# A two-layer diffusion backbone in fp32: the opening's scales and shifts summed together, its first up weights loaded in pairs

## The chip, the cores and the metric

The kernel runs on one core of one Trainium2 chip. The metric is the device time of one execution in microseconds; lower is better. All matrix products are done in fp32 precision, each by three products of rounded parts: a high part (fp32r, what the engine rounds to) and a low part, the difference.

## The reference, cut to what matters

```python
for l in range(DEPTH):                       # DEPTH = 2, D_MODEL = 1024, D_FF = 2816
    mod_x = adaln_params(c, w_mod[l], b_mod[l])          # silu(c) @ w_mod + b_mod, 9 sections of 1024
    mod_c = adaln_params(c_ctx[None], w_mod[l], b_mod[l])
    x   = ffn_sublayer(x,   mod_x, 0, norm_w[l, 0], ffn1_w_up[l], ffn1_w_down[l])   # 256 latent tokens
    ctx = ffn_sublayer(ctx, mod_c, 0, norm_w[l, 0], ffn1_w_up[l], ffn1_w_down[l])   # 256 context tokens
    ...                                                  # retention and convolution branches, second FFN
return rmsnorm(x, final_norm_w)

def modulated_norm(h, w, mod, i):
    return rmsnorm(h, w) * (1.0 + mod[:, :, 3 * i + 1]) + mod[:, :, 3 * i]

def ffn_sublayer(h, mod, i, norm_w, w_up, w_down):
    y = modulated_norm(h, norm_w, mod, i)
    a, b = jnp.split(y @ w_up, 2, axis=-1)
    return h + 0.5 * mod[:, :, 3 * i + 2] * ((jax.nn.silu(a) * b) @ w_down)
```

Only the opening matters here: the norm's scale (section 1) and shift (section 0) of layer 0, which two vector-by-matrix products give, then `y`, then the first columns of `y @ w_up`.

## The kernel before

The program is straight-line code for five queues. Activations lie transposed: `H`, `XN` and `Y` hold 8 blocks `k` of 128 channels, each 512 columns wide (256 latent tokens, then 256 context tokens). `Y[:, k, 0]` is the high part, `Y[:, k, 1]` the low one. A "unit" is a block of 1024 x 128 weights (512 KB); unit `cc` of the up stage is column block `cc // 2` of the first or the second half of `w_up`, and sums into PSUM bank `cc`. SyncE loads a unit into `RAW`, ScalarE copies its high part to `HI` (line 1095), VectorE subtracts and writes `LO` over `RAW` (line 1560), and TensorE runs 24 matmuls, three for each `k`: HI by Y high, HI by Y low, LO by Y high. There are six slots for units.

The stage "ada" is the opening. SyncE issues the inputs, then 16 pieces of `w_mod` (`load_mod(b)`, line 568, 512 KB each) and the first four up units, in one queue. Four groups `g` cover two blocks `k` each; the pieces of group `g` are `4g` and `4g + 1` (scale) and `4g + 2` and `4g + 3` (shift). TensorE's `modulation(b)` (line 844) multiplies a piece by `SCW`, the activated condition widened by zeros, so that 128 rows hold four partial sums for two conditions. ScalarE's `rows_out` (line 1236) copies the rows of one section out of bank 4 or 5, TensorE's `columns` (line 854) sums and turns them into columns, and VectorE's `mods0` (lines 1790 and 1796) adds the bias and forms the scale `AMUL`. Then `y0` on ScalarE (line 1244) writes the high part of `Y` for both conditions, `y0_full` and `y0_low` on VectorE (lines 1806, 1813) the low part. `xn` (line 1819) multiplies `H` by the inverse root. `h_copy` (1250 on ScalarE, 1827 on VectorE) copies the turned inputs out of the eight banks, block 7 out of bank 3. `keep_clock(n)` (line 811) runs `n` matmuls of ones whose result nobody reads.

The order of each queue is written out by hand. On TensorE `first_units(ks, units)` (lines 868 and 872) runs blocks `ks` of some of the four units among the modulation pieces. Units 2 and 3 run their blocks 6 and 7 last, after units 0 and 1 are complete. After the opening comes the stage "up" with units 4 to 43; there ScalarE applies Silu to unit 0 (line 1292) before it rounds unit 4, and a unit's load waits until the last user of its slot is complete. Everything downstream (down projection, retention, convolution, second layer) is not touched.

## Time and profile before

| | |
|---|---|
| median of 3 runs | 2137.32 us (2135.09 to 2137.92) |
| the profiled execution | 2135.14 us |
| its span | 2133.4 us |
| TensorE busy | 2121.3 us (99%) |
| VectorE busy | 1431.6 us (67%) |
| ScalarE busy | 804.5 us (38%) |
| mean transfer rate | 149 GB/s |
| first matmul of unit 4 | 56.88 us |

All times within the execution are microseconds from the start of the span. A timeline row gives the start, the duration, the engine (PE is TensorE, PEld its weight loads, DVE is VectorE, ACT is ScalarE), the line, the operation with its output and input, and in brackets the idle time before it with what ended it. A fp32 matmul shows as two passes (x2), and the shown end of a matmul reaches beyond the start of the next, so spacing between starts is what a matmul costs. What lies between the span and the time of the execution, 1.7 us, is start and end outside the queues.

### The profile page before, as it was taken

The numbers are of one execution on the slowest core, as the hardware profiler recorded it, in microseconds if no ns is written. First come the engines' busy times: TensorE is split into PE (matmuls) and PEld (weight loads), VectorE is DVE, ScalarE is ACT, GpSimd is POOL, SyncE is SP. The second block draws the span as 40 slices with busy tenths as digits, with TensorE's granted clock in tenths as the row PEclk, the third lists the DMA queues.
The fourth block names the chain that finished last, engine by engine and source line by source line (L and its number), as shares of the span: only waits on it lengthen the run. The fifth ranks groups of instructions, "written<-read, shape, count | busy, mean of one in ns | idle before, by whom it ended". The sixth has DMA issues, their size and how long they took to land.

```text
span 2133.4 us, 26488 instructions
## 1 busy us (share of the span) xinstructions
PE 2121.3 (99%) x10747; PEld 1803.4 (85%) x10747; DVE 1431.6 (67%) x1965; ACT 804.5 (38%) x1194; POOL 0.2 (0%) x4
## 2 busy tenths in 40 slices
PE   9999999999999999999999999999999999999998
PEld 7888888988888888888888888888889888888887
DVE  5677777659588773477777767733335688777765
ACT  4322222455322322342222233222223665556654
POOL 0000000000000000000000000000000000000000
PEclk9999999999999999999999999999999999999999
DMA  8655555431555543355555544433333447775664
GB/s 262 197 170 175 160 166 161 126 99 41 157 158 158 172 154 99 89 149 163 172 168 161 169 135 144 133 98 99 92 99 107 133 116 199 206 212 144 188 190 146
DMA packets 454398, 318.17 MB, mean 149 GB/s; under 512 B 10478, under 2 KB 429702, under 8 KB 453894
## 3 DMA queue, kind: packets, MB, share of 16 engines
q1 hardware_dynamic: 432476, 243.43, 39.3%
q10 hardware_dynamic: 21800, 73.03, 10.0%
q8 instruction: 86, 1.41, 0.3%
q14 instruction: 36, 0.29, 0.0%
HBM read 312.23 MB, written 1.05 MB: 147 GB/s over the span
## 4 chain that ended last, share of the span: by engine, by line
PE 97%; SPq 1%; DVE 1%; DMA 0%; ACT 0%; issue 0%; DVEq 0%
PE bank L645 23%; PE bank L647 23%; PE bank L646 23%; PE bank L656 9%; PE bank L659 5%; PE bank L963 4%; PE bank L691 2%; PE bank L727 1%; PE bank L725 1%; PE bank L726 1%; PE bank L695 1%; SPq L568 1%; PE bank L868 1%; PE bank L801 0%; DMA RAW<-in_ffn_w_up_dram 0%; PE bank L1007 0%
## 5 line engine op out<-in xcount | busy, mean ns | idle before, releaser
L1560 DVE TENSOR_TENSOR LO<-RAW,HI 128x1024 fp32r<-128x1024 f32 (+1 forms) x435 | 523.1, 1207 | 341.0 <-ACT HI L1095 340.9
L645 PE MATMUL bank<-Y,HI 128*128 128x512 f32 (+1 forms) x1440 | 555.7, 386 | 0.0
L647 PE MATMUL bank<-Y,LO 128*128 128x512 f32 (+1 forms) x1440 | 553.6, 384 | 0.0
L646 PE MATMUL bank<-Y,HI 128*128 128x512 f32 (+1 forms) x1440 | 553.5, 384 | 0.0
L1095 ACT ACTIVATE HI<-RAW 128x1024 fp32r<-128x1024 f32 (+1 forms) x435 | 441.5, 1039 | 141.5 <-DMA RAW<-in_w_in_dram 52.2
L645 PEld LDWEIGHTS bank<-Y,HI 128*128 128x128 f32 x1440 | 270.6, 188 | 54.2 <-issue 1.3
L647 PEld LDWEIGHTS bank<-Y,LO 128*128 128x128 f32 x1440 | 270.5, 188 | 53.9
L646 PEld LDWEIGHTS bank<-Y,HI 128*128 128x128 f32 x1440 | 270.6, 188 | 53.6 <-issue 0.5
L1571 DVE SCALAR_TENSOR_TENSOR MODACC<-MODRAW,SC,MODACC 128x1024 f32<-128x1024 f32 x224 | 277.2, 1279 | 2.4 <-DMA MODRAW<-in_w_mod_dram 2.0
L645 PE MATMUL bank<-Z,HI 128*128 128x512 f32 (+1 forms) x594 | 218.0, 367 | 0.0
L647 PE MATMUL bank<-Z,LO 128*128 128x512 f32 (+1 forms) x594 | 217.1, 366 | 0.0
L646 PE MATMUL bank<-Z,HI 128*128 128x512 f32 (+1 forms) x594 | 217.1, 365 | 0.0
L1292 ACT ACTIVATE TMP<-bank 128x512 f32<-128x512 f32 x66 | 39.5, 598 | 457.0 <-PE bank L647 373.5
L656 PE MATMUL bank<-Y,HI 128*128 128x512 f32 x720 | 181.0, 393 | 0.0
L656 PEld LDWEIGHTS bank<-Y,HI 128*128 128x128 f32 x720 | 129.6, 189 | 23.3
L645 PEld LDWEIGHTS bank<-Z,HI 128*128 128x128 f32 x594 | 112.0, 189 | 18.2
L646 PEld LDWEIGHTS bank<-Z,HI 128*128 128x128 f32 x594 | 112.0, 189 | 18.1
L647 PEld LDWEIGHTS bank<-Z,LO 128*128 128x128 f32 x594 | 112.0, 189 | 17.9
L1680 DVE SCALAR_TENSOR_TENSOR H<-bank,GATE,H 128x256 f32<-128x256 f32 x64 | 28.3, 479 | 121.7 <-PE bank L647 121.7
L659 PEld LDWEIGHTS bank<-Y,LO 128*128 128x128 f32 x720 | 98.2, 190 | 7.0
L659 PE MATMUL bank<-Y,LO 128*128 128x256 f32 x720 | 100.4, 282 | 0.0
L1889 DVE TENSOR_TENSOR TMP<-bank,TMP 128x512 f32<-128x512 f32 x66 | 45.5, 690 | 75.7 <-PE bank L647 75.7
(290 smaller groups left out, 2468.2 us busy)
## 6 DMA issues: line engine op xcount, KB each, us to landing
RAW<-in_ffn_w_up_dram SPq DMA_DIRECT2D x174, 512.0 KB, 3.8
MODRAW<-in_w_mod_dram ACTq DMA_DIRECT2D x128, 512.0 KB, 4.4
RAW<-in_w_in_dram SPq DMA_DIRECT2D x128, 512.0 KB, 4.0
RAW<-in_ffn_w_down_dram SPq DMA_DIRECT2D x66, 512.0 KB, 3.9
RAW<-in_ffn_w_down_dram SPq DMA_DIRECT2D x24, 384.0 KB, 3.4
WM<-in_w_mod_dram SPq DMA_DIRECT2D x16, 512.0 KB, 8.3
RAW<-in_w_ret_out_dram SPq DMA_DIRECT2D x16, 512.0 KB, 4.1
RAW<-in_w_conv_out_dram SPq DMA_DIRECT2D x16, 512.0 KB, 4.0
```

Of the source, the lines that this page charges most:

```text
L645: mm(bank, hi, X[:, k, 0, cols], start=first, stop=False)
L646: mm(bank, hi, X[:, k, 1, cols], start=False, stop=False)
L647: return mm(bank, lo, X[:, k, 0, cols], start=False, stop=end)
L656: mm(halves2(bank[:]), wblock(u, 0, k), X[:, k, :, cols], start=(k == 0), stop=False)
L659: ins = mm(bank[:, 0:HALF], wblock(u, 1, k), X[:, k, 0, cols], start=False, stop=(k == KT - 1))
L691: mm(B[cc][:, cols], wblock(s.u + cc, part, k), Y[:, k, 0, cols], start=(k == 0 and part == 0), stop=False)
L963: ins = mm(B[s.acc[4 * half + tt].bank][:], Y[:, k, a, tt * P:(tt + 1) * P], weights(u, w)[:, kk * 512:(kk + 1) * 512], start=(k == 0 and ...
L1095: A(weights(v, 0), raw_weights(v), ACT.Copy).then_inc(hi_done, 1)
L1292: A(TMP[:, o % 2, cols], B[s.acc[cc].bank][:, cols], ACT.Silu).then_inc(drained[s.acc[cc].bank], 1)
L1560: V_.tensor_tensor(weights(v, 1), raw_weights(v), weights(v, 0).bitcast(F32), ALU.subtract).then_inc(lo_done, 1)
L1571: V_.scalar_tensor_tensor(acc, MODRAW[i % 2][:], a, acc, ALU.mult, ALU.add).then_inc(mod_step, 1)
L1889: V_.tensor_tensor(TMP[:, 2 + o % 2, cols], B[s.acc[cc].bank][:, cols], TMP[:, o % 2, cols], ALU.mult).then_inc(drained[s.acc[cc].bank], 1)
```

## The change

Six things change, all in the opening.

- Scale and shift of a group are summed in the same rows: `SCW` has a copy of the condition for each section, two columns apart, and all four pieces of a group accumulate in one bank (4 or 5 by turns). One `rows_out`, one `columns` (which yields four columns for each block) and one `mods0` serve a group.
- The first four up units are loaded as two pairs of 1 MB, (0, 2) and (1, 3). A pair holds two neighbouring column blocks of one half of `w_up`, 1 KB a row. The first pair is issued behind pieces 0 to 3, the second behind pieces 4 to 7. Low parts are written over the pair, with a stride.
- TensorE sweeps unit by unit: unit 0 and unit 2 on blocks 0 and 1, then pieces 4 to 7, then units 0, 2, 1 and 3 as listed; in `one_unit` all products with the high weights come first, then those with the low weights. Blocks 4 to 7 run over all four units together (`all_units`).
- In ScalarE's queue a unit's rounding stands between blocks of `y0`.
- In VectorE's queue the copies of blocks 5 and 7 and the second block's scaling stand behind the low part of block 0.
- The dummies: 3, 2, 2 and 8 in place of 3, 5, 3, 2 and 5. The wait for bank 3 stands before the last ones in both.

```diff
@@ plan
-            s.rows = [[p.acc(4), p.acc(5)] for g in range(4)]
-            s.cols_acc = [[p.acc(6), p.acc(7)] for g in range(4)]
+            s.rows = [p.acc(4 + g % 2) for g in range(4)]
+            s.cols_acc = [p.acc(7 - g % 2) for g in range(4)]
...
+    for i, pair in enumerate(PAIRS):                  # PAIRS = ((0, 2), (1, 3))
+        for e, u in enumerate(pair):
+            p.slot[u], p.prior[u], p.landed[u], p.pair[u] = u, None, 16, (i, e)
+        user[2 * i] = user[2 * i + 1] = pair[1]
@@ SyncE
-                    load_mod(0)
-                    load_mod(1)
-                    load_up(0)
...
-                    load_up(3)
+                    def load_pair(i):
+                        sp.dma_start(RAWP[i][:], wu.rearrange("(k p) n -> p k n", p=P)[:, :, i * FF:i * FF + 2 * P]
+                                     ).then_inc(raw_landed[2 * i], 16)
+                    for b in range(4):
+                        load_mod(b)
+                    load_pair(0)
+                    for b in range(4, 8):
+                        load_mod(b)
+                    load_pair(1)
                     for b in range(8, 16):
                         load_mod(b)
@@ TensorE
+                    def one_unit(cc, ks):
+
+                        n = [u for pair in PAIRS for u in pair].index(cc)
+                        if 0 in ks:
+                            bank_wait(pe, up_s.acc[cc])
+                            pe.wait_ge(hi_done, n + 1)
                         for k in ks:
                             pe.wait_ge(y0_hi, 2 * k + 2)
...
+                            mm(B[cc][:], wblock(cc, 0, k), Y[:, k, 0, :], start=(k == 0), stop=False)
                             pe.wait_ge(y0_lo, k + 1)
...
+                            mm(B[cc][:], wblock(cc, 0, k), Y[:, k, 1, :], start=False, stop=False)
+                        if 0 in ks:
+                            pe.wait_ge(lo_done, n + 1)
+                        for k in ks:
+                            ins = mm(B[cc][:], wblock(cc, 1, k), Y[:, k, 0, :], start=False, stop=(k == KT - 1))
...
                     modulation(0)
                     drain_wait(pe, s.turn[0])
                     keep_clock(3, s.turn[0].bank)
...
-                    columns(0, 1)
                     drain_wait(pe, s.turn[6])
-                    keep_clock(5, s.turn[6].bank)
                     modulation(2)
-                    keep_clock(3, s.turn[6].bank)
+                    keep_clock(2, s.turn[6].bank)
                     modulation(3)
                     keep_clock(2, s.turn[6].bank)
-                    columns(0, 0)
+                    columns(0)
                     drain_wait(pe, s.turn[7])
-                    keep_clock(5, s.turn[7].bank)
-                    first_units((0, 1), (0,))
...
-                    first_units((6, 7), (3,))
+                    keep_clock(8, s.turn[7].bank)
+                    one_unit(0, (0, 1))
+                    one_unit(2, (0, 1))
+                    for b in range(4, 8):
+                        modulation(b)
+                    columns(1)
+                    one_unit(0, (2, 3))
+                    one_unit(2, (2, 3))
+                    one_unit(1, (0, 1, 2, 3))
+                    one_unit(3, (0, 1))
                     for b in range(8, 12):
                         modulation(b)
...
+                    one_unit(3, (2,))
+                    columns(2)
+                    one_unit(3, (3,))
+                    all_units(4, range(4))
                     for b in range(12, 16):
                         modulation(b)
...
+                    all_units(5, (0, 1))
+                    columns(3)
+                    all_units(5, (2, 3))
+                    all_units(6, range(4))
+                    all_units(7, range(4))
@@ ScalarE
-                    h_copy(0, 1, 3)
...
-                    y0(5, 6, 7)
+                    h_copy(0, 1, 3, 6)
+                    rows_out(0)
+                    y0(0)
+                    pair_hi(0)
+                    y0(1)
+                    pair_hi(2)
+                    rows_out(1)
                     y0(2, 3)
...
+                    pair_hi(1)
+                    pair_hi(3)
+                    split_at[0] = 4
+                    rows_out(2)
+                    y0(4, 5)
+                    rows_out(3)
+                    y0(6, 7)
@@ VectorE
-                    xn(0, 1)
-                    mods0(0, 1)
-                    h_copy(5, 7)
-                    split_upto(0)
-                    mods0(0, 0)
+                    xn(0)
+                    mods0(0)
                     y0_full(0)
                     y0_low(0)
+                    xn(1)
+                    h_copy(5, 7)
+                    pair_lo(0)
                     y0_full(1)
                     y0_low(1)
-                    split_upto(2)
...
+                    pair_lo(2)
+                    xn(2, 3, 4, 5)
+                    mods0(1)
...
```

## Rows read from the trace of the kernel before

**Rows 1.** The page, part 1: busy time and share by engine.

```profile
PE 2121.3 (99%) x10747; PEld 1803.4 (85%) x10747; DVE 1431.6 (67%) x1965; ACT 804.5 (38%) x1194; POOL 0.2 (0%) x4
```

**Rows 2.** Busy by engine (instructions), clock, transfer share, GB/s, by stretch.

```profile
20.00:25.00 5.00, 4.25 (x24) 2.95 (x24) 4.30 (x9) 3.37 (x6) 0.00 (x0) 1.00 1.13 327
35.00:40.00 5.00, 5.00 (x45) 3.58 (x47) 3.58 (x7) 0.35 (x2) 0.00 (x0) 1.00 1.10 350
50.00:55.00 5.00, 5.00 (x24) 4.12 (x23) 1.65 (x3) 3.57 (x6) 0.00 (x0) 1.00 0.00 1
60.00:65.00 5.00, 5.00 (x24) 4.14 (x23) 3.00 (x5) 2.92 (x4) 0.00 (x0) 1.00 1.11 346
60.00:500.00 440.00, 439.97 (x2154) 373.37 (x2153) 317.91 (x411) 149.39 (x208) 0.00 (x0) 1.00 0.49 151
```

**Rows 3.** Chain of waits, opening: start, duration, what.

```profile
22.45 8.06 DMA RAW<-in_ffn_w_up_dram
...
30.54 1.06 ACT HI L1095
...
32.02 0.58 PE bank L854 x4
```

**Rows 4.** Timeline of TensorE, 19 to 57 us.

```profile
19.25 0.64 PE L844 MATMUL bank<-WM,SCW 128*32 128x256 f32 x8
...
20.49 0.58 PE L854 MATMUL bank<-CK,ADAROWS 128*128 128x2 f32 x4
20.93 1.36 PE L811 MATMUL bank<-ONES 128*128 128x128 f32 x10
22.59 0.47 PE L868 MATMUL bank<-Y,HI 128*128 128x512 f32 x1 [0.30 <-ACT Y L1244]
...
42.84 1.93 PE L844 MATMUL bank<-WM,SCW 128*32 128x256 f32 x32
44.71 0.50 PE L868 MATMUL bank<-Y,HI 128*128 128x512 f32 x1
...
53.50 0.62 PE L872 MATMUL bank<-Y,HI 128*128 128x512 f32 x2
...
56.44 0.39 PE L872 MATMUL bank<-Y,HI 128*128 128x512 f32 x1
56.88 0.47 PE L645 MATMUL bank<-Y,HI 128*128 128x512 f32 x1
```

**Rows 5.** Issues from 3.0 to 3.2 us in flight, median to landing.

```profile
WM<-in_w_mod_dram SPq DMA_DIRECT2D x2, 512.0 KB, 10.9
```

**Rows 6.** Timeline of VectorE, 10 to 22 us.

```profile
10.00 1.23 DVE L1821 SCALAR_TENSOR_TENSOR TMP<-XROWS 128x1024 f32<-128x1024 f32 x1 [2.63 <-DMA XROWS<-in_ctx_dram]
...
18.57 1.28 DVE L1827 COPY H<-bank 128x512 f32<-128x512 f32 x2
19.77 1.22 DVE L1560 TENSOR_TENSOR LO<-RAW,HI 128x1024 fp32r<-128x1024 f32 x1
21.10 0.16 DVE L1790 TENSOR_TENSOR MODS<-bank,VT 128x4 f32<-128x4 f32 x1
```

**Rows 7.** Timeline of ScalarE, 12 to 22 us.

```profile
12.03 1.55 ACT L1250 ACTIVATE H<-bank 128x512 f32<-128x512 f32 x3
...
21.35 2.08 ACT L1244 ACTIVATE Y<-XN,MODS,AMUL 128x256 fp32r<-128x256 f32 x4 [1.01 <-DVE MODS L1790]
```

**Rows 8.** Up loads issued from 50 to 70 us: issue to landing.

```profile
DMA to landing us min/median/max: 3.9/5.2/6.5
```

**Rows 9.** Columns as in the second group, the program's end.

```profile
2127.00:2128.00 1.00, 0.43 (x4) 0.23 (x2) 0.88 (x3) 0.51 (x2) 0.00 (x0) 1.00 0.00 0
...
2131.00:2132.00 1.00, 0.00 (x0) 0.00 (x0) 0.00 (x0) 0.00 (x0) 0.00 (x0) 0.77 1.02 381
```

**Rows 10.** Dummies' weight loads from 0.9 to 3.9 and 5 to 8 us.

```profile
L811 PEld LDWEIGHTS bank<-ONES x14: 288/333/333, 1.0 to 3.8; 128*128 128x128 f32 x14
...
L811 PEld LDWEIGHTS bank<-ONES x25: 186/192/290, 4.8 to 8.0; 128*128 128x128 f32 x25
```

More of the change, by code:

```diff
@@ L48, in constants @@
     keep[:, CK_QS:CK_QS + P] = (p[:, None] % 32 == p[None, :] % 32)
-    keep[p % 32 == 0, CK_COMB] = 1.0
-    keep[p % 32 == 1, CK_COMB + 1] = 1.0
+    for row in range(4):
+        keep[p % 32 == row, CK_COMB + row] = 1.0
     mix = np.zeros((P, CM_W), np.float32)
@@ L75 @@
 V_SPARE = (2, 4)
+PAIRS = ((0, 2), (1, 3))
 class Acc:
@@ L105, in __init__ @@
         self.total_acc = {}
-        self.slot, self.prior, self.landed = {}, {}, {}
+        self.slot, self.prior, self.landed, self.pair = {}, {}, {}, {}
     def acc(self, bank):
@@ L298, in plan @@
             u = s.u + c
+            if u in p.pair:
+                continue
             slot = (u + (rows and s.kind in ("up", "down"))) % SLOTS
@@ L361, in build @@
     CROWS = place("CROWS", [2 * KT, P], F32, zone + 82944)
[L362 to L363 removed]
+    ADAROWS = place("ADAROWS", [P, 2, GROUP], F32, zone + 83968)
+    SCW = place("SCW", [P, KT, 2, 32], F32, zone + 88064)
     DIAG = place("DIAG", [P, 512], F32, zone + 94208)
@@ L369, in build @@
     RAW = [place(f"RAW{s}", [P, UW], F32, cursor[0] + 4 * UW * s) for s in range(SLOTS)]
+    RAWP, LOP = [[place(f"{n}{i}", [P, KT, 2 * P], dt, cursor[0] + 8 * UW * i) for i in range(2)]
+                 for n, dt in (("RAWP", F32), ("LOP", F32R))]
     LO = [place(f"LO{s}", [P, UW], F32R) for s in range(SLOTS)]
@@ L460, in weights @@
             slot = pl.slot[u]
+            if u in pl.pair:
+                i, e = pl.pair[u]
+                return (HI[slot][:].rearrange("p (k n) -> p k n", k=KT), LOP[i][:, :, e * P:(e + 1) * P])[part]
             if slot < SLOTS:
@@ L468, in wblock @@
             slot = pl.slot[u]
+            if u in pl.pair and part:
+                i, e = pl.pair[u]
+                return LOP[i][:, kk, e * P:(e + 1) * P]
             if slot < SLOTS:
@@ L480, in raw_weights @@
             slot = pl.slot[u]
+            if u in pl.pair:
+                i, e = pl.pair[u]
+                return RAWP[i][:, :, e * P:(e + 1) * P]
             if slot < SLOTS:
@@ new lines, in one_unit, with all_units @@
+                        if 0 in ks:
+                            pe.wait_ge(lo_done, n + 1)
+                        for k in ks:
+                            ins = mm(B[cc][:], wblock(cc, 1, k), Y[:, k, 0, :], start=False, stop=(k == KT - 1))
+                        if KT - 1 in ks:
+                            ins.then_inc(unit_done, 1)
+                    def all_units(k, units):
+                        pe.wait_ge(y0_hi, 2 * k + 2)
+                        for cc in units:
+                            for part in range(2):
+                                mm(B[cc][:], wblock(cc, part, k), Y[:, k, 0, :], start=False, stop=False)
+                        pe.wait_ge(y0_lo, k + 1)
+                        for cc in units:
+                            ins = mm(B[cc][:], wblock(cc, 0, k), Y[:, k, 1, :], start=False, stop=(k == KT - 1))
+                            if k == KT - 1:
+                                ins.then_inc(unit_done, 1)
@@ L1776, in _ @@
             dve.wait_ge(small_set, 4)
-            V_.tensor_copy(SCW[:, :, 0:2], SC[:].rearrange("p c k -> p k c")).then_inc(sc_wide, 1)
+            for sec in range(2):
+                V_.tensor_copy(SCW[:, :, sec, 2 * sec:2 * sec + 2], SC[:].rearrange("p c k -> p k c")).then_inc(sc_wide, 1)
             for s in stages:
@@ L1800, in y0_full, with pair_lo @@
+                    def pair_lo(cc):
+                        dve.wait_ge(hi_done, [u for pair in PAIRS for u in pair].index(cc) + 1)
+                        V_.tensor_tensor(weights(cc, 1), raw_weights(cc), weights(cc, 0).bitcast(F32), ALU.subtract
+                                         ).then_inc(lo_done, 1)
                     def y0_full(*ks):
                         for k in ks:
-                            drain_wait(dve, s.cols_acc[k // 2][0])
+                            dve.wait_ge(mods0_done, k // 2 + 1)
+                            dve.wait_ge(xn_done, k + 1)
```

152 lines of the change are left out of this document (48 added, 104 removed).

## The prediction, written before the change was run

> **What bounds the kernel now.** I read the busy shares first, then TensorE's clock and the transfers in five-microsecond stretches, then the chain of waits through the opening, and last the timelines of the three engines, one against another. TensorE is busy 99% of the span [rows 1], so nearly nothing is to be won outside the first 57 us, and whatever TensorE loses or gains there is passed on to the end at its full size: from 60 to 500 us it is idle for 0.03 us [rows 2]. In the opening the transfers run at 327 to 350 GB/s and are idle from 50 to 55 us, while TensorE works without a gap [rows 2]. So the opening is bound by transfers only in its first half. The chain says where it changes hands: the fourth up block lands at 30.5 us, is rounded and subtracted, and lets the second group's sums go on at 32.0 us [rows 3]. From 35 us on TensorE has no gap [rows 2] until 0.2 us before unit 4 begins at 56.88 us [rows 4]. The reader should see that the last transfers of the modulation weights are not what is waited for: TensorE comes to them at 42.84 us from other work, not from a wait.
>
> From 22.59 to 56.67 us TensorE spends 34.1 us. Of this, 96 matmuls of the first four units cost 96 x 0.227 = 21.8 us (thirteen steps from 53.50 to 56.44 are 0.226 each [rows 4], with the first of a group a little longer); twelve modulation pieces cost 12 x 0.465 = 5.6 (four take 1.87, from 42.84 to 44.71 [rows 4]); six turnings cost 6 x 0.44 = 2.6. The rest, about 4.1 us, is waiting. A change that removed all waiting and two turnings' worth could not bring much over 4 us; that is the whole prize.
>
> **The change, part by part.** I follow the new order with the old durations.
>
> Small edits first. SCW has twice the columns: one memset 0.27 us longer and one more copy of 0.18 on VectorE, which then idles 2.63 us for the context rows [rows 6]; nothing, and 0.45 us if that cover were gone. The number of weight transfers is the same; four blocks of 512 KB become two of 1 MB whose rows are twice as long. ScalarE writes out four sums in place of eight (0.38 us each), TensorE turns four times, which saves 4 x 0.44 = 1.8 us, 1.3 of it after the first unit begins. VectorE's small sums stay twelve.
>
> *Transfers.* All issues sit in SyncE's queue; no waiting instruction lies among them. Piece 3 now lands ahead of any up block, the first pair follows, pieces 4 to 7 come before the second pair. The mixed stretches run at 327 GB/s, the one with modulation weights alone at 350 [rows 2]; with a third of the bytes in up blocks that is 289 GB/s for an up block, 1.8 us against 1.5. But 60 to 65 us carries up blocks mainly and runs at 346. So a block in a pair costs between 1.5 and 1.8 us. The Trainium skill, "DMA: Bandwidth & Descriptors", Specifications, gives full rate from runs of 512 B upward; by it the pairs would win nothing, and the first mixed stretches here do not bear that out. Either way the first pair lands at 20.3 to 20.9 us: the first two pieces take 10.9 us from issue in the median [rows 5], so the second, issued at 3.1, is in at about 14.2, and two pieces of 1.5 and the pair follow. ScalarE asks for it only at 21.2: no effect on the sum.
>
> *The opening to the first scale.* The first piece now goes to bank 4, which ScalarE frees with its third copy at 13.58 [rows 7] rather than with its second, so it starts 0.5 us later, at 13.7. Then: 0.57 for the piece, 0.87 for three dummies, 0.57, then 0.96 for the broadcast of the inverse roots: piece 2 begins at 16.65 and piece 3 at 17.8, instead of 19.25, since five dummies and one turning are gone and it has landed (17.3). From piece 3's start to the first small sum took 1.85 us (19.25 to 21.10 [rows 4, 6]): 19.65. The three small sums end at 20.1. ScalarE writes the first Y at 20.2 (now 21.35 [rows 7]): 1.1 us gained.
>
> *The gap that this opens.* TensorE ends its only turning at 19.6. Its next instruction waits for bank 3, which VectorE frees with the copy of block 7. Today that copy is done at 19.8 [rows 6]. In the new order it stands behind the full and the low part of block 0 and the scaling of block 1. The low part waits for ScalarE's two halves, half of 2.08 us [rows 7], until 21.3. A pass of VectorE over 512 columns takes 0.6 to 0.7 us (two copies 1.28 [rows 6]). Low part, scaling and two copies, 2.5 us: bank 3 is free at 23.8. TensorE is idle from 19.6 to 23.9, 4.3 us. Then eight dummies, 16 passes of 0.136 us (ten take 1.36 [rows 4]), 2.2 us: the first unit begins at 26.1, not at 22.6. VectorE meanwhile goes on to unit 0's low weights (23.75, 1.14), block 1 full and low (0.66, 0.69): 26.2, unit 2's low weights to 27.4. So without the dummies unit 0 would still end only 0.4 us earlier; the order on VectorE holds it too. High parts first hides only the low weights, not block 1. Cost: 3.5 us in the start. Strided reads of a pair have no row; the engines take 1.06 and 1.22 us for 1024 elements in a row [rows 3, 6], and I take these; between 0 and +0.5 us.
>
> *The middle.* Units 0 and 2 on two blocks: 12 x 0.227, to 28.8. Pieces 4 to 7 (landed by 27): to 30.7. Sum out, turned, small sums: 30.7 + 0.1 + 0.38 + 0.1 + 0.6 + 0.5 = 32.4, then 1.0 on ScalarE for block 2, and TensorE has its block at 33.4. Idle 2.3 us, with no unit queued behind it. Unit 0 on blocks 2 and 3 waits for each part in turn, 1.4 us more. At 36.2 everything is there; unit 2 (1.4), unit 1 (2.7), unit 3 (1.4), pieces 8 to 11 (1.9): 43.5. Three matmuls, the turning at 44.2, three matmuls, 45.3. Block 4 is ready 2.2 us after its turning starts (0.6 to the first small sum as from 20.49 to 21.10, 0.5 for the three, 1.1 for ScalarE's two halves [rows 4, 6, 7]); today four pieces cover that. It waits to 46.4: 1.1 us. Twelve matmuls, pieces, half of block 5 and the last turning: 52.8. Half of block 5 covers 1.4 of the 1.8 us after it; 0.4 us idle. Blocks 6 and 7: the last matmul ends its turn at 60.1. Check as a sum: 26.1 + 21.8 + 5.6 + 1.3 + (2.3 + 1.4 + 1.1 + 0.4) = 60.0. Now it is 56.67: +3.4 us. Bounds of the four waits together: 1.2 us less (small handovers cost 0.1 rather than 0.4), 1 us more.
>
> *The end of the opening.* ScalarE rounds unit 4's weights only behind the Silu of unit 0, and VectorE subtracts behind that. From the start of unit 0's last matmul (53.50) to unit 4's first (56.88) is 3.4 us [rows 4]. Now twelve matmuls of units 2 and 3 lie in between and the gap is 0.2. In the new order all four units end together, three matmuls after unit 0: 0.9 us of cover from that start. TensorE is idle 2.5 us: +2.3 (1.9 to 2.7). The transfers of units 6 to 9 now wait for units 2 and 3, that is for 59.9 us; they take 3.9 to 6.5 us to land [rows 8], ScalarE and VectorE 2.3 more, and unit 6 is due 10.9 us after unit 4's start, at 73.5. Cover about 5 us; no cost, and 1 us of waiting for each us by which it is exceeded. The earlier table load on ScalarE (1.28) ends well before.
>
> Sum: +3.4 + 2.3 = +5.7 us. The profiled execution took 2135.14 us around its span of 2133.4; it would become 2140.8. The median of the three runs is 2137.32, 2.2 higher, so the forecast is **2143.0 us**, its own range +4.4 to +6.9 and 1 us of spread on both sides.
>
> **Rivals.** *The clock falls in the gap.* At the end of the program TensorE stops at 2127.4, and the granted clock over 2131 to 2132 is 0.77, so that it fell to 1.2 GHz about the middle of it, some 4.1 us after the last matmul [rows 9]. My gap is 4.3 us, good to some 0.3, hardly longer than that one, and matmuls that begin in time would keep the clock: a third of the cases in which the gap is there. At the program's start weight loads of dummies take 333 ns up to 3.8 us and 192 from 4.8 on [rows 10], the low level and 2.4 GHz, and 13 of them start between 1.0 and 3.8, 0.215 each. Sixteen dummy passes then cost 16 x 0.215 in place of 16 x 0.136, +1.3, and one unit matmul doubles: +1.5, in all +7.2, 2144.5. The Trainium skill, "TensorE: Matmul & The Clock Gate", Part 1, calls the half rate the state after idling; the end of the trace agrees.
>
> *Transfers set the opening after all.* If the last piece, not TensorE, holds the end of the opening, the end moves with its landing, 1.2 us earlier, and only the tail is paid: +1.1, 2138.4. A mixture (half of the gaps covered) gives +3. Against it: no TensorE gap after 35 us now.
>
> *Faster.* If bank 3 is free early and VectorE is not what holds block 1, the first unit starts with the first Y, at 21.4: 21.4 + 28.7 + 1.5 of waits = 51.6, plus 2.5 of tail = 54.1 against 56.88: -2.8, 2134.5. With no waits at all it is -4.3. It decides from where VectorE's copy of block 7 is done before 20 us; the diff puts it behind block 0. *The change doesn't do what it says*: the up blocks are needed so late that their order is without effect; it gives the transfers' case.
>
> **How the numbers follow.** A measurement can tell about 0.2%, 4.3 us. Forecast 0.43, clock 0.2, transfers or mixture 0.27, faster 0.10. Slower by over 0.2%: most of the first (0.39) and all of the second, 0.59. Within: 0.04 of the first, the third, and 0.05 of the faster case, 0.36. Faster: the other 0.05. The range goes from the transfers' case less 1 us of spread, 2137.3, to the clock case with its waits at their upper bound, 2146.5.
>
> **What would show it.** In the new profile: TensorE idle some 4 us before the eight dummies, released by VectorE's copy of H; first unit matmul near 26; gaps of about 2, 1 and 0.5 us before blocks 2, 4 and 6; unit 4 about 3.4 us after unit 0's last matmul starts, at 62.6; dummies of 16 passes in 2.2 us (3.4 if the clock fell). The forecast is wrong if bank 3 is free before 20 us, or if unit 4 begins before 60 us.

## The result, and the profile after

The changed kernel takes 2147.35 us in the median (2145.71 to 2148.07, six runs); the kernel before, on the same chip, 2135.72 (2135.09 to 2137.92). The ratio is 1.005, with a 95% interval of 1.004 to 1.006: slower by 11.6 us. The forecast was slower by 5.7 us, 2143.0; the sign and the places are right, the size is half of the measured one, and the measured median lies 0.85 us above the stated range. The forecast stood on a median of 2137.32 us for the kernel before; counted from there the range reached to +9.2 us, so in differences the measured 11.6 lies 2.4 us beyond it.

The profiled execution took 2145.71 us, its span 2143.9, 10.5 more than before. All of that is there when unit 4 begins: 67.41 us against 56.88 [rows 4], also 10.5. What follows lasts 2076.49 us, before 2076.52. TensorE's timeline of the opening (columns as ahead, L860 is the modulation, L870 the turning, L827 the dummies, L882 to L900 the first four units, L661 unit 4):

```profile
13.39 0.64 PE L860 MATMUL bank<-WM,SCW 128*32 128x256 f32 x8 [1.33 <-ACT H L1274]
...
17.66 0.64 PE L860 MATMUL bank<-WM,SCW 128*32 128x256 f32 x8
...
18.89 0.58 PE L870 MATMUL bank<-CK,ADAROWS 128*128 128x4 f32 x4
23.71 3.78 PE L827 MATMUL bank<-ONES 128*128 128x128 f32 x16 [4.24 <-DVE H L1857]
27.15 0.77 PE L882 MATMUL bank<-Y,HI 128*128 128x512 f32 x1
...
30.60 1.93 PE L860 MATMUL bank<-WM,SCW 128*32 128x256 f32 x32
33.12 0.58 PE L870 MATMUL bank<-CK,ADAROWS 128*128 128x4 f32 x4 [0.59 <-ACT ADAROWS L1257]
35.42 0.80 PE L882 MATMUL bank<-Y,HI 128*128 128x512 f32 x1 [1.72 <-ACT Y L1268]
...
39.04 0.63 PE L882 MATMUL bank<-Y,HI 128*128 128x512 f32 x1
...
41.60 0.52 PE L882 MATMUL bank<-Y,HI 128*128 128x512 f32 x1
...
45.95 1.93 PE L860 MATMUL bank<-WM,SCW 128*32 128x256 f32 x32
...
50.84 0.50 PE L897 MATMUL bank<-Y,HI 128*128 128x512 f32 x1 [0.90 <-ACT Y L1268]
...
59.37 0.50 PE L897 MATMUL bank<-Y,HI 128*128 128x512 f32 x1 [0.21 <-ACT Y L1268]
...
64.04 1.07 PE L900 MATMUL bank<-Y,HI 128*128 128x512 f32 x4
67.41 0.47 PE L661 MATMUL bank<-Y,HI 128*128 128x512 f32 x1 [2.31 <-DVE LO L1582]
```

The gap is where it was forecast: the turning stands at 18.89 [rows 4: 20.49], then TensorE idles 4.24 us, released by VectorE's copy of `H`. Three more gaps follow, before block 2 (1.72 us), block 4 (0.90) and block 6 (0.21), and one of 2.31 us before unit 4, released by `LO`. Two things are not in the forecast's main case. The dummies take 3.44 us to the next start where 16 x 0.136 = 2.2 were reckoned, and the six matmuls from 39.04 to 41.60 start 0.43 us apart where 0.227 was reckoned [rows 4].

The order on VectorE that holds bank 3 (L1857 copies blocks 5 and 7):

```profile
21.16 0.69 DVE L1843 TENSOR_TENSOR Y<-TMP,Y 128x512 fp32r<-128x512 f32 x1 [0.39 <-ACT Y L1268]
21.77 0.68 DVE L1849 TENSOR_TENSOR XN<-H,RB 128x512 f32<-128x512 f32 x1
22.38 1.28 DVE L1857 COPY H<-bank 128x512 f32<-128x512 f32 x2
23.57 1.22 DVE L1826 TENSOR_TENSOR LOP<-RAWP,HI 128x1024 fp32r<-128x1024 f32 x1
24.71 0.73 DVE L1836 TENSOR_SCALAR TMP<-XN,AMUL,MODS 128x256 f32<-128x256 f32 x2
25.54 0.69 DVE L1843 TENSOR_TENSOR Y<-TMP,Y 128x512 fp32r<-128x512 f32 x1
```

The copies end at 23.66, today's at 19.85 [rows 6]. The low part of block 1, on which unit 0's second block waits, ends at 26.2.

TensorE's clock, by stretch (columns as in [rows 2]; the clock is the number behind the POOL column):

```profile
20.50:21.00 0.50, 0.00 (x0) 0.00 (x0) 0.28 (x1) 0.50 (x2) 0.00 (x0) 1.00 1.07 356
21.00:21.50 0.50, 0.00 (x0) 0.00 (x0) 0.34 (x1) 0.50 (x2) 0.00 (x0) 0.88 1.10 358
21.50:22.00 0.50, 0.00 (x0) 0.00 (x0) 0.50 (x2) 0.50 (x1) 0.00 (x0) 0.50 1.10 346
28.00:28.20 0.20, 0.20 (x2) 0.10 (x2) 0.20 (x1) 0.00 (x0) 0.00 (x0) 0.50 1.10 348
28.20:28.40 0.20, 0.20 (x2) 0.17 (x1) 0.20 (x1) 0.00 (x0) 0.00 (x0) 0.97 1.10 348
...
34.80:35.00 0.20, 0.00 (x0) 0.00 (x0) 0.20 (x1) 0.20 (x2) 0.00 (x0) 1.00 1.10 348
...
35.10:35.30 0.20, 0.00 (x0) 0.00 (x0) 0.00 (x0) 0.20 (x2) 0.00 (x0) 0.50 1.10 343
41.60:41.70 0.10, 0.10 (x2) 0.10 (x1) 0.00 (x0) 0.00 (x0) 0.00 (x0) 0.50 1.06 256
```

It fell to 1.2 GHz at about 21.4 us, was back at 2.4 GHz at 28.2, fell again at 35.0 and was back at 41.9. The first fall comes 1.9 us after the last matmul (19.47), not 4.1 as at the program's end [rows 9]. The second comes 1.3 us after the end of the turning at 33.7, ahead of which TensorE had waited 0.59 us. In both cases TensorE had been at work again for some time, 4.5 and 6.4 us, before the clock was back.

### The profile page after: what moved, and what is told of

Read it like the earlier page. It is cut to its first block, busy times and chain, and to the rows that moved or that the text cites. A ratio compares the mean times of both kernels' runs of the same rounds, so it can differ in the third digit from the quotient of the medians.

```text
span 2143.9 us, 26434 instructions
## 1 busy us (share of the span) xinstructions
PE 2123.6 (99%) x10725; PEld 1804.1 (84%) x10725; DVE 1431.6 (67%) x1966; ACT 803.6 (37%) x1190; POOL 0.2 (0%) x4
## 3 DMA queue, kind: packets, MB, share of 16 engines
q10 hardware_dynamic: 21800, 73.03, 10.3%
## 4 chain that ended last, share of the span: by engine, by line
PE 98%; DVE 1%; ACT 1%; issue 0%; DVEq 0%; ACTq 0%
PE bank L661 23%; PE bank L663 23%; PE bank L662 23%; PE bank L672 9%; PE bank L675 5%; PE bank L984 4%; PE bank L707 2%; PE bank L742 1%; PE bank L743 1%; PE bank L741 1%; PE bank L711 1%; PE bank L827 1%; PE bank L817 0%; PE bank L860 0%; PE bank L1028 0%; PE bank L1030 0%
## 5 line engine op out<-in xcount | busy, mean ns | idle before, releaser
L661 PE MATMUL bank<-Y,HI 128*128 128x512 f32 (+1 forms) x1440 | 555.7, 386 | 2.3 <-DVE LO L1582 2.3
L661 PEld LDWEIGHTS bank<-Y,HI 128*128 128x128 f32 x1440 | 270.6, 188 | 56.6 <-issue 3.5
L661 PE MATMUL bank<-Z,HI 128*128 128x512 f32 (+1 forms) x594 | 218.0, 367 | 0.0
L661 PEld LDWEIGHTS bank<-Z,HI 128*128 128x128 f32 x594 | 112.0, 189 | 18.1
```

What stands on the lines that cost most here:

```text
L661: mm(bank, hi, X[:, k, 0, cols], start=first, stop=False)
```

## The experiments

The start moves by up to 1.1 us from one execution to the next (ScalarE's first copy of `H` starts at 11.70 to 12.82 us), and with it the first modulation piece (13.19 us before, 13.35 to 14.47 in the kernels below). So I compare, beside the medians, the time from the first piece to unit 4: 43.69 us in the kernel before (56.88 less 13.19), 54.02 in the changed kernel. This measure leaves out one part of the change. With the joint sums the first piece waits for ScalarE's third copy and not for its second, and starts 1.65 us after the first copy and not 1.16:

```profile
11.74 2.04 ACT L1274 ACTIVATE H<-bank 128x512 f32<-128x512 f32 x4
```

Against the kernel before, the joint sums thus look 0.5 us better by this measure than they are. From ScalarE's first copy to unit 4 the two kernels take 44.85 us (56.88 less 12.03 [rows 7]) and 55.67. The medians of the kernel before beside these runs were 2135.7 to 2136.6.

### Copies of blocks 5 and 7 early

```diff
-                    h_copy(4)
+                    h_copy(4, 5, 7)
...
                     xn(1)
-                    h_copy(5, 7)
                     pair_lo(0)
```

> The changed kernel with one edit: VectorE's copies of blocks 5 and 7 stand behind its copy of block 4, where it idles from 13.8 to 16.5 us, not behind the low part of block 0. Theory (order on VectorE and the clock): bank 3 is free before 16 us, the eight dummies follow the turning at once, the clock stays at 2.4 GHz through the first gap, the first unit begins at about 22.2 us instead of 27.15, pieces 4 to 7 at 27 instead of 30.6, and unit 4 at 60.8 us if the clock does not fall in the gap behind the second turning either, at 62.8 if it does (67.41 in the changed kernel): 4.6 to 6.6 us faster, 2140.7 to 2142.8. Rival (the late start is made up anyway, the loss lies in the sweep and the end of the opening): less than 1.5 us.

Measured: 2145.24 us, 1.0046 of the kernel before (1.003 to 1.0063), 2.1 us faster than the changed kernel; first piece to unit 4 52.11 us. Both theories miss: the gain is less than half of the 4.6 us that the first one gave at least, and more than the rival's 1.5. The eight dummies do follow at once, but the clock fell all the same. The timeline and the clock of this kernel:

```profile
20.41 2.03 PE L827 MATMUL bank<-ONES 128*128 128x128 f32 x16
23.27 0.47 PE L882 MATMUL bank<-Y,HI 128*128 128x512 f32 x1 [0.82 <-ACT HI L1261]
...
24.79 0.49 PE L882 MATMUL bank<-Y,HI 128*128 128x512 f32 x1 [0.82 <-ACT Y L1268]
26.18 0.49 PE L884 MATMUL bank<-Y,HI 128*128 128x512 f32 x1 [0.90 <-DVE Y L1843]
```

```profile
25.00:26.00 1.00, 0.28 (x1) 0.00 (x0) 0.90 (x3) 0.68 (x1) 0.00 (x0) 1.00 1.11 348
...
27.00:28.00 1.00, 1.00 (x4) 0.80 (x3) 1.00 (x3) 0.00 (x0) 0.00 (x0) 0.59 1.10 347
28.00:29.00 1.00, 1.00 (x4) 0.66 (x2) 1.00 (x3) 0.00 (x0) 0.00 (x0) 0.50 1.10 346
```

Unit 0 goes on block by block, and each waits: 0.82, 0.82 and 0.90 us, none longer. TensorE was busy 0.28 of the microsecond from 25. The clock fell at 27.2 us, when TensorE had been at work again without a pause since 26.18. A gap of 4 us is thus not needed, and matmuls that begin again in time did not keep the clock. The gap behind the second turning (1.72 us) is still there, and the clock fell a second time at 34.0 us.

### Dummies in the gaps, all other queues as in the changed kernel

```diff
+                    keep_clock(16, s.turn[6].bank)
                     drain_wait(pe, s.turn[7])
                     keep_clock(8, s.turn[7].bank)
...
                     columns(1)
+                    keep_clock(8, s.turn[7].bank)
```

> The changed kernel with dummies where TensorE idles: sixteen on bank 2 ahead of the wait for bank 3 (4.3 us of work in a gap of 4.24), eight on bank 3 behind the second turning (2.2 us in a gap of 1.7). All waits and orders on the other engines stay. If the clock is worth what the trace says (two stretches at 1.2 GHz, 21.4 to 28.2 and 35.0 to 41.9 us), the granted clock is 1.00 throughout and unit 4 begins at 62.6 to 63.2 us instead of 67.41: 4.2 to 4.8 us faster, 2142.5 to 2143.1. If the low clock only fills time in which TensorE would have waited, less than 1 us.

Measured: 2144.15 us, 1.0038 (1.0023 to 1.0053); first piece to unit 4 49.96 us, 4.06 less than in the changed kernel. The clock is 1.00 from 18 to 64 us, as expected. The saving in the median is only 3.2 us, and in the profiled execution the clock fell at the gap before unit 4:

```profile
63.00:64.00 1.00, 0.00 (x0) 0.00 (x0) 1.00 (x1) 1.00 (x2) 0.00 (x0) 1.00 0.60 172
64.00:65.00 1.00, 0.70 (x2) 0.64 (x3) 1.00 (x3) 0.54 (x2) 0.00 (x0) 0.73 1.09 327
65.00:66.00 1.00, 1.00 (x4) 0.71 (x4) 0.88 (x1) 0.42 (x1) 0.00 (x0) 0.50 1.17 334
...
67.00:68.00 1.00, 1.00 (x4) 0.78 (x3) 0.78 (x1) 0.28 (x2) 0.00 (x0) 0.56 1.20 291
```

It is not the first gap without dummies: waits of 0.59, 0.69 and 0.90 us stand ahead of it. Unit 4 begins at 64.30 and the clock falls about 0.2 us later. In the changed kernel TensorE waits just as long before unit 4, 2.31 us, after the same matmuls, and the clock holds:

```profile
64.00:70.00 6.00, 3.69 (x16) 2.74 (x16) 3.09 (x4) 4.67 (x6) 0.00 (x0) 1.00 0.69 187
```

So the same gap can cost the clock in one execution and not in another; what decides between them is not shown. One of the four runs took 2141.72 us, 2.4 us less than the other three; it was not profiled. From unit 4 to the end takes 2078.1 us here and 2076.5 to 2076.7 in the others, 1.6 us at the price of slow matmuls.

What follows: the two stretches at 1.2 GHz cost the changed kernel 4.1 us, about half each. Pieces 4 to 7 begin 15.16 us after the first piece here (29.50 less 14.34) and 17.21 in the changed kernel (30.60 less 13.39), 2.05 us later; the rest comes behind them.

### Unit 4 split ahead of the Silu of unit 0

```diff
@@ ScalarE
                     y0(6, 7)
+                    split_upto(4)
@@ VectorE
                     y0_low(7)
+                    split_upto(4)
```

> The changed kernel with one edit: ScalarE rounds unit 4 behind its last y0 and VectorE subtracts it behind the last low part, ahead of the Silu of unit 0. Theory: the 2.31 us in which TensorE waits for unit 4's low part are gone, unit 4 begins at 65.0 to 65.2 us, 2.2 to 2.4 us faster, 2145.0. Rival: bank 0, freed only behind the Silu of unit 0, is waited for in its place; unit 0 is complete 0.7 us before the end and the Silu takes 0.6, so a wait of up to 0.5 us stays and the gain is 1.8.

Measured: 2144.71 us, 1.0043 (1.0028 to 1.0058), 2.6 us faster than the changed kernel. The gap before unit 4 is gone, and no wait for bank 0 took its place:

```profile
60.60 0.50 PE L897 MATMUL bank<-Y,HI 128*128 128x512 f32 x1 [0.21 <-ACT Y L1268]
...
66.34 0.50 PE L661 MATMUL bank<-Y,HI 128*128 128x512 f32 x1
```

From the start of block 6 to unit 4 it is 5.74 us; in the changed kernel 8.04 (59.37 to 67.41). So the end of the opening cost 2.3 us, as forecast. First piece to unit 4 is 52.29 us, only 1.73 less than in the changed kernel. The waits ahead of block 6 are the same, the first one 4.24 us again, but the clock kept another time:

```profile
22.00:26.00 4.00, 1.63 (x7) 1.63 (x8) 4.00 (x7) 2.78 (x4) 0.00 (x0) 0.61 1.10 348
```

By this row it fell at about 22.9 us, 2.8 us after the last matmul (20.13), where it had fallen after 1.9, and pieces 4 to 7 begin 17.55 us after the first piece and not 17.21. The price of the clock is thus not the same in every execution of the same opening.

### The kernel before with the copies late

```diff
                     mods0(0, 1)
-                    h_copy(5, 7)
                     split_upto(0)
                     mods0(0, 0)
                     y0_full(0)
                     y0_low(0)
+                    h_copy(5, 7)
```

> The kernel before with one edit: the copies of blocks 5 and 7 stand behind the low part of block 0. Theory: bank 3 is free at 24.3 us, TensorE idles from 21.1, the clock falls in the gap, and the first unit begins at 26 to 27 us instead of 22.59. The kernel before waits for the fourth up block until 32.0 anyway, so of 3.5 to 4.5 us only part comes through: unit 4 at 58.9 to 61, 2 to 4 us slower. Rival (a late start costs nothing, since transfers bound the first half): within 0.5 us.

Measured: 2138.53 us, 1.0012 (1.0003 to 1.0022), 2.8 us slower than the kernel before; first piece to unit 4 46.95 us, 3.3 more. The same gap opens in the kernel before:

```profile
25.01 2.50 PE L811 MATMUL bank<-ONES 128*128 128x128 f32 x10 [3.35 <-DVE H L1827]
27.16 0.77 PE L868 MATMUL bank<-Y,HI 128*128 128x512 f32 x1
```

The clock is 0.67 from 22 to 26 us and 0.50 from 26 to 30. The place of two copies of 0.6 us in VectorE's queue is worth 3 us with the low clock that the gap brings, since they hold a bank for which the dummies wait. Part of it is absorbed by the wait for the fourth up block, 1.24 us before the second group's turning in the kernel before and 0.59 here.

### Dummies and unit 4 together

The edits of the second and the third experiment.

> The changed kernel with the dummies of the second experiment (sixteen on bank 2 ahead of the wait for bank 3, eight on bank 3 behind the second turning) and unit 4 split ahead of the Silu of unit 0. If clock and tail are two separate terms, they add up: 2.3 us for the tail and 1.6 for the slow matmuls behind it off the 2144.15 us of the dummies alone, 2140.3 us, granted clock 1.00 everywhere before the end. What is then left over the kernel before, some 4.5 us, is the waiting that the order itself makes (block 1 behind three other jobs on VectorE, the gaps behind the turnings). Rival (the low clock only moves to another place): above 2142.

Measured: 2140.05 us, 1.0019 (1.001 to 1.0029); first piece to unit 4 47.66 us, 2.30 less than with the dummies alone. The terms add up, and 4.0 us are left over the kernel before.

### Another order, the joint sums and the pairs kept

```diff
@@ TensorE
                     columns(0)
                     drain_wait(pe, s.turn[7])
-                    keep_clock(8, s.turn[7].bank)
+                    keep_clock(12, s.turn[7].bank)
...
+                    keep_clock(2, s.turn[7].bank)
                     columns(1)
+                    keep_clock(7, s.turn[7].bank)
                     one_unit(0, (2, 3))
                     one_unit(2, (2, 3))
                     one_unit(1, (0, 1, 2, 3))
-                    one_unit(3, (0, 1))
                     for b in range(8, 12):
                         modulation(b)
-                    one_unit(3, (2,))
+                    one_unit(3, (0,))
                     columns(2)
-                    one_unit(3, (3,))
+                    one_unit(3, (1, 2, 3))
                     all_units(4, range(4))
                     for b in range(12, 16):
                         modulation(b)
-                    all_units(5, (0, 1))
+                    all_units(5, (0,))
                     columns(3)
-                    all_units(5, (2, 3))
+                    all_units(5, (1, 2, 3))
@@ ScalarE
-                    y0(0)
-                    pair_hi(0)
-                    y0(1)
+                    y0(0, 1)
+                    pair_hi(0)
                     pair_hi(2)
@@ VectorE (copies of 5 and 7 early, unit 4 split early, as above)
-                    xn(0)
+                    xn(0, 1)
...
-                    xn(1)
-                    pair_lo(0)
                     y0_full(1)
                     y0_low(1)
+                    pair_lo(0)
                     pair_lo(2)
```

> The changed kernel's sums and pairs with another order: copies of blocks 5 and 7 early; blocks 0 and 1 of Y ahead of the splitting of units 0 and 2; twelve dummies ahead of unit 0, two ahead of the second turning and seven behind it; pieces 8 to 11 ahead of unit 3, one block of unit 3 ahead of the third turning and three behind it, pieces 12 to 15, one quarter of block 5 ahead of the last turning and three behind it; unit 4 split early. Theory (the loss is order and clock, not the joint sum and not the pairs): no wait over 0.3 us behind the third and fourth turning, clock 1.00, unit 4 at 56 to 57.5 us counted from a first piece at 13.4, so 2135 to 2137.5 us, level with the kernel before. Rival (the joint sum itself costs, since one late turning stands where two stood): 2139 or more.

Measured: 2136.38 us, ratio 1.0 (0.999 to 1.0009), level with the kernel before; first piece to unit 4 43.96 us, and the clock is 1.00. Behind the third and the fourth turning TensorE no longer waits. From ScalarE's first copy to unit 4 it is 45.61 us, 0.8 more than in the kernel before, half of it and more the later first piece. Joint sums and pairs can thus stand in a kernel that is not measurably slower.

### The joint sum alone, in the kernel before

```diff
-            s.rows = [[p.acc(4), p.acc(5)] for g in range(4)]
-            s.cols_acc = [[p.acc(6), p.acc(7)] for g in range(4)]
+            s.rows = [p.acc(4 + g % 2) for g in range(4)]
+            s.cols_acc = [p.acc(7 - g % 2) for g in range(4)]
...
-                    columns(0, 1)
...
-                    columns(0, 0)
+                    columns(0)
```

and so for `SCW`, `modulation`, `rows_out` and `mods0`, as in the change; loads, sweep and dummies stay.

> The kernel before with one part of the change: scale and shift of a group summed in the same rows and turned at once. Loads, sweep, dummies, VectorE's and ScalarE's order as before. Theory: four turnings of 0.44 us go, three of them after the first unit began, the first piece starts 0.3 us later; unit 4 at 55.5 to 56.5 us, 0.5 to 1.5 us faster than the kernel before, 2134.2 to 2135.2. Rival (the joint sum needs all four pieces before any small sum, so each scale is ready later): 1 to 2 us slower.

Measured: 2135.16 us, ratio 0.9998 (0.9988 to 1.0007); first piece to unit 4 42.88 us, 0.8 less than in the kernel before. Of this 0.8 us, 0.5 is the later start of the first piece, which waits for ScalarE's third copy; from ScalarE's first copy to unit 4 it is 44.53 us, 0.3 less than before. So most of what four turnings fewer save is paid back at the start, and the rest can't be told from no change in the time.

### The pairs as single transfers

```diff
-                        sp.dma_start(RAWP[i][:], wu.rearrange("(k p) n -> p k n", p=P)[:, :, i * FF:i * FF + 2 * P]
-                                     ).then_inc(raw_landed[2 * i], 16)
+                        for e in range(2):
+                            sp.dma_start(RAWP[i][:, :, e * P:(e + 1) * P],
+                                         wu.rearrange("(k p) n -> p k n", p=P)[:, :, i * FF + e * P:i * FF + (e + 1) * P]
+                                         ).then_inc(raw_landed[2 * i + e], 16)
```

> The changed kernel with each pair loaded as two transfers of one unit, 512 B a row, in the same place of the queue. If rows of 512 B are what slows the mixed stretches (327 GB/s before, 348 in the changed kernel), the stretch from 20 to 35 us falls to about 327 to 335 GB/s and the last piece lands 0.7 to 1 us later; the time is the changed kernel's within 1 us, since no wait of TensorE ends with a transfer. Rival (the order of transfers made the rate): 348 GB/s as in the changed kernel.

Measured: 2146.98 us, 1.0051 (1.0036 to 1.0066), the changed kernel's time; first piece to unit 4 54.24 us. The transfers of this kernel and then of the changed one, the last number in GB/s:

```profile
15.00:20.00 5.00, 4.70 (x40) 2.34 (x38) 1.62 (x4) 0.38 (x1) 0.00 (x0) 1.00 1.15 307
20.00:25.00 5.00, 1.06 (x5) 1.06 (x6) 4.51 (x9) 4.07 (x6) 0.00 (x0) 0.70 1.06 342
25.00:30.00 5.00, 5.00 (x22) 4.50 (x22) 4.89 (x9) 0.00 (x0) 0.00 (x0) 0.62 1.15 306
```

```profile
15.00:20.00 5.00, 4.47 (x38) 2.18 (x30) 1.77 (x5) 0.38 (x1) 0.00 (x0) 1.00 1.11 349
...
25.00:30.00 5.00, 5.00 (x22) 4.49 (x22) 4.67 (x8) 0.00 (x0) 0.00 (x0) 0.68 1.10 348
```

With rows of 512 B the stretches that carry up blocks run at 306 to 307 GB/s, with rows of 1 KB at 348 to 349. The pairs do raise the rate, and it buys nothing here: no wait of TensorE ends with a transfer. TensorE's waits are those of the changed kernel (4.24, 0.59, 1.72, 0.90, 0.21 and 2.30 us). The row from 20 us shows the clock once more: it fell at about 22.0, 2.3 us after the last matmul (19.70).

### Early copies with the dummies and unit 4

The kernel of the fifth experiment, with `h_copy(4, 5, 7)` as in the first and `keep_clock(12, s.turn[7].bank)` in place of sixteen and eight.

> The kernel of the dummies and the early unit 4, with the copies of blocks 5 and 7 early as well and twelve dummies ahead of unit 0 in place of sixteen and eight. It prices VectorE's order with the clock held up. Theory: two copies (1.2 us) leave the chain ahead of the low part of block 1, pieces 4 to 7 begin 1.2 us earlier than 15.15 us after the first piece, and everything behind them too: 2138.9 us against 2140.05. Rival (the clock falls in the short waits inside units 0 and 2, as it did with early copies alone): no gain or a loss.

Measured: 2140.81 us, 1.0019 (1.001 to 1.0028); first piece to unit 4 48.15 us, 0.5 more than in the fifth; the ratio to the kernel before is the fifth's. The rival holds in the profiled execution:

```profile
25.00:30.00 5.00, 4.26 (x17) 2.85 (x21) 4.23 (x6) 0.24 (x1) 0.00 (x0) 0.66 1.10 349
```

Between the twelve dummies and the pieces 4 to 7 units 0 and 2 wait for blocks and low parts (0.82 and 0.91 us), and the clock is 0.66 from 25 to 30 us. One of eleven runs took 2138.37 us, near the 2138.9 of the theory; it was not profiled. So VectorE's order has no price of its own that this pair of kernels shows; it is known only together with the rest of the sixth experiment.

### The second pair ahead of pieces 6 and 7

```diff
@@ SyncE
-                    for b in range(4, 8):
+                    for b in range(4, 6):
                         load_mod(b)
                     load_pair(1)
-                    for b in range(8, 16):
+                    for b in range(6, 16):
                         load_mod(b)
@@ TensorE (from the reordered kernel)
                     one_unit(0, (0, 1))
                     one_unit(2, (0, 1))
-                    for b in range(4, 8):
-                        modulation(b)
+                    modulation(4)
+                    modulation(5)
+                    one_unit(1, (0, 1))
+                    modulation(6)
+                    modulation(7)
                     keep_clock(2, s.turn[7].bank)
                     columns(1)
-                    keep_clock(7, s.turn[7].bank)
+                    one_unit(3, (0, 1))
...
```

with `pair_hi` and `pair_lo` of units 1 and 3 ahead of the second group on ScalarE and VectorE, and units 1 and 3 on blocks 2 and 3 around the third turning.

> The reordered kernel with the second pair loaded ahead of pieces 6 and 7, units 1 and 3 on blocks 0 and 1 put where it ran dummies, and the turnings covered as there. Theory: the second pair lands at about 26 us, unit 1 and unit 3 take 2.7 us out of the stretch after block 2's arrival, which comes at most 0.3 us later, so unit 4 starts 2 to 2.7 us earlier than in the reordered kernel (41.3 to 42 us after the first piece in place of 43.96): 2133.7 to 2134.5 us, 1.5 to 2.3 us faster than the kernel before. Rival (piece 7 comes a pair later and all behind it too): level with the reordered kernel, 2136.4.

Measured: 2135.56 us, ratio 0.9997 (0.9988 to 1.0006). First piece to unit 4 is 43.54 us, 0.4 less than in the reordered kernel and not 2 or more. The expectation's error was that block 2 comes at most 0.3 us later:

```profile
13.63 0.64 PE L860 MATMUL bank<-WM,SCW 128*32 128x256 f32 x8 [1.38 <-ACT H L1278]
...
31.59 0.58 PE L870 MATMUL bank<-CK,ADAROWS 128*128 128x4 f32 x4
...
33.89 0.50 PE L882 MATMUL bank<-Y,HI 128*128 128x512 f32 x1 [0.23 <-ACT Y L1272]
```

```profile
14.39 0.64 PE L860 MATMUL bank<-WM,SCW 128*32 128x256 f32 x8 [1.50 <-ACT H L1275]
...
30.05 0.58 PE L870 MATMUL bank<-CK,ADAROWS 128*128 128x4 f32 x4
...
32.34 0.50 PE L882 MATMUL bank<-Y,HI 128*128 128x512 f32 x1
```

Block 2 starts 20.3 us after the first piece here and 18.0 in the reordered kernel. The chain of waits leads to it through the second pair: it lands at 26.86 us and not at 26, is rounded from 26.88 and subtracted from 27.98, unit 1's products with the low weights start at 29.26, and pieces 6 and 7, which stand behind them in TensorE's queue, at 29.92:

```profile
26.88 2.01 ACT L1265 ACTIVATE HI<-RAWP 128x1024 fp32r<-128x1024 f32 x2 [2.62 <-DMA RAWP<-in_ffn_w_up_dram]
```

Piece 7 itself lands only at 29.9 (issued at 20.7, 9.2 us to landing). So the pair's place in SyncE's queue and unit 1's place in TensorE's both hold block 2 back, and took the gain of filling the gap. No version is measurably faster than the kernel before.

## Why the prediction was right and where it was not

The terms, from first piece to unit 4, by the kernels that take them away one at a time: changed kernel 54.02 us; without the low clock 49.96; without the wait for unit 4 as well 47.66; with the other order 43.96; the kernel before 43.69. So of 10.3 us the clock has 4.1, the end of the opening 2.3, the order of the queues 3.7, and 0.3 stays for the rest. From ScalarE's first copy the loss is 10.8 us and the rest 0.8, since the later first piece is in it.

**What bounds the kernel.** Right. The whole difference arises ahead of unit 4 and is passed on at its full size (2076.49 and 2076.52 us behind it).

**Transfers.** Right in the sum: no effect. The rate was at the upper of the stated bounds; the first pair landed at 19.9 us (issue at 7.7 plus 12.2), a little ahead of the 20.3. The prediction's lower bound, 289 GB/s for a block with rows of 512 B, was the right figure for such blocks, and its second reading was wrong: the stretch from 60 to 65 us of the kernel before, 346 GB/s [rows 2], does not carry up blocks mainly. From 58 to 62 us up blocks run alone, in packets of 512 B, at 288 to 293 GB/s; from 62.5 to 64.5 the loads of ScalarE's queue, in packets of some 4 KB, run at 402, and the average hides both. Modulation pieces, transfers of the same 512 KB with rows of 1 KB, run at 350. So it is the row width, not the number of transfers. What the Trainium skill, "DMA: Bandwidth & Descriptors", Specifications, states, full rate from 512 B upward, does not hold here: 288 to 293 GB/s at 512 B alone, 306 to 307 mixed with rows of 1 KB, 348 to 350 at 1 KB.

**The opening and the gap.** Right, within 0.3 us at each step: ScalarE's first `Y` at 20.04 (forecast 20.2), bank 3 free at 23.66 (23.8), TensorE's gap 4.24 us (4.3), low part of block 1 at 26.2 (26.2). The copies' place in the queue is shown as a cause from the other side: put late in the kernel before, they cost 2.8 us, the low clock included.

**The middle.** Right in its parts: TensorE waits 0.59 us before the second turning and 1.72 behind it, together the 2.3 that were reckoned, then 0.90 and 0.21 where 1.1 and 0.4 were. In unit 0 on blocks 2 and 3, 1.4 us of waiting were reckoned; the trace has 0.22 at the low clock, and 0.23 and 0.69 with the clock held up. The start and the middle together were put at +3.4, 0.5 of it the later first piece. With the clock held up they are 4.0 from the first piece and 4.5 from ScalarE's first copy (49.31 less 44.85), some 1 us more than reckoned; no single wait has it.

**The end of the opening.** Right: a gap of 2.31 us (forecast 2.5, less the 0.2 there before), and 2.3 us came back when unit 4 was split ahead.

**The clock.** This is the step that failed, by size and by chance. The fall in the gap was made a rival with one chance in three and a price of 1.5 us, from one row at the program's end, where the clock held 4.1 us past the last matmul [rows 9]. The prediction read that row as the time a gap must last, and reckoned that matmuls which begin in time keep the clock. Both readings are wrong. In three executions with this same gap of 4.24 us (the changed kernel, the third and the eighth experiment) the clock fell 1.9, 2.8 and 2.3 us after the last matmul. At the gap before unit 4 of the second experiment, and within unit 0 of the first, it fell when matmuls had begun again.

The price was too low as well. One fall was put at 1.5 us; the first one cost 2.05. The part that was reckoned, the dummies and the first matmul, came out right (the dummies take 3.44 us, the 16 x 0.215 of the rival, and the first unit starts 1.6 us later than with the clock held), but the clock was back only at 28.2 and the next matmuls were slow too. And it was priced as one event. The clock fell a second time, at 35.0 us, and stayed down until 41.9, through units 0 and 2. The two stretches together cost 4.1 us, as the dummies show. Without the clock the forecast was +5.7; measured it is 49.96 less 43.69, +6.3 (+6.8 from ScalarE's first copy), within its own range of +4.4 to +6.9. With the clock it is +10.3 (+10.8). So the main case was right in its mechanism and nearly in its size, and it was the clock, its second fall above all, that made the sum half of what was measured.

The Trainium skill, "TensorE: Matmul & The Clock Gate", Part 1, calls the half rate the state after idling. The first fall agrees with it; the first fall of the first experiment and the one of the ninth came where no wait was longer than 0.91 us. Why the clock falls at one such place and not at another (the sixth and tenth experiments have waits of 0.91 and 0.69 us at 1.00) is not shown.

**The rivals.** "Transfers set the opening" is out: no wait of TensorE ends with a transfer, and slower transfers left the time as it was. "Faster" asked for bank 3 to be free early and for VectorE not to hold block 1. With the first alone (the first experiment) the kernel stays 9.5 us slower. With copies early, order changed and clock kept, unit 4 comes at the same distance as in the kernel before (43.96 and 43.54 against 43.69; from ScalarE's first copy 0.8 and 0.4 us later), not 2.8 us earlier.

## What to carry to other kernels

An instruction that only frees a buffer has its due time too: before a copy is moved behind others on its engine, look for who waits for the bank, dummies included. When a sweep is changed so that several units end together, count again what stood between the first one's end and the next unit's operands; here 2.3 us of cover were lost and came back by two moved instructions. Price a gap of TensorE in an opening twice, for itself and for the low clock behind it, and price every gap. One row in which the clock held through a gap is no sign that the next gap is safe: in these runs the same gap of 2.3 us cost the clock once and left it alone in the others, and waits of 0.8 to 0.9 us in a row cost it twice. When a rate of transfers is read from a stretch, look first at whether one kind of transfer fills it.

## What the runs showed of the hardware that was not expected

How long the granted clock holds after the last matmul varied in the same order of instructions: 1.9, 2.3 and 2.8 us behind the first turning of the changed kernel in three executions, 1.7 in the fourth experiment, and 4.1 at the end of the program. Dense work ahead does not settle it. Before unit 4 of the second experiment matmuls of 512 columns had run for some 7.6 us with one wait of 0.2, and the clock fell 2.5 us after the last of them, 0.2 us into the next; in the changed kernel the same gap left it at 1.00. It also fell where TensorE never waited longer than 0.91 us, once when matmuls had been running again for 1.0 us.

In the changed kernel it was low from 21.4 to 28.2 us and from 35.0 to 41.9, and came back only 4.5 and 6.4 us after matmuls had begun again. Matmuls of 512 columns then start 0.43 us apart and not 0.227, a dummy's passes 0.215 and not 0.136. Dummies in the two gaps held the clock at 1.00 from 18 to 64 us.

Loads from memory with rows of 512 B ran at 288 to 293 GB/s where nothing else was under way, those with rows of 1 KB at 348 to 350.
